# Down projections of a split-precision block: one 512-column product in place of two of 256

## The reference, cut to what matters

```python
def swiglu(x, w_gate, w_up, w_down):
    return (jax.nn.silu(x @ w_gate) * (x @ w_up)) @ w_down
...
def first_block(x, ...):
        h = rms_norm(x, ffn1_norm[l])
        x = x + FFN_RESIDUAL_WEIGHT * swiglu(h, ffn1_w_gate[l], ffn1_w_up[l], ffn1_w_down[l])   # f1u, f1d
...
        h = rms_norm(x, ffn2_norm[l])
        x = x + FFN_RESIDUAL_WEIGHT * swiglu(h, ffn2_w_gate[l], ffn2_w_up[l], ffn2_w_down[l])   # f2u, f2d
    return rms_norm(x, final_norm)
...
def second_block(x, mem, ...):
        fn = rms_norm_2(h, norm_ffn[l])
        g = fn @ ffn_w_gate[l]
        ...
        h = h + (jax.nn.silu(g_conv) * (fn @ ffn_w_up[l])) @ ffn_w_down[l]                      # f3u, f3d
    return h
```

## Time and profile before

| | before |
|---|---|
| median of 3 runs | 965.79 us |
| the profiled execution | 965.9 us |
| its span, first to last instruction | 964.2 us |
| TensorE matmul busy | 958.1 us (99%), 8272 matmuls |
| VectorE busy | 690.8 us (72%) |
| ScalarE busy | 535.0 us (55%) |
| GpSimd busy | 129.8 us (13%) |
| granted TensorE clock | 1.000 of full speed |

### The profile page before, as it was taken

The page is one execution under the profiler, slowest core; times in us unless marked ns, Lnnn a source line. Parts: engine busy times, 40 slices in busy tenths (PEclk is TensorE's granted clock), DMA queues, the critical chain, the costliest instruction groups (busy, mean ns, idle before and its releaser), DMA issues.

```text
span 964.2 us, 20474 instructions
## 1 busy us (share of the span) xinstructions
PE 958.1 (99%) x8272; PEld 941.5 (98%) x8272; DVE 690.8 (72%) x1084; ACT 535.0 (55%) x777; POOL 129.8 (13%) x85
## 2 busy tenths in 40 slices
PE   9999999999999999999999999999999999999998
PEld 8999999999999999999999999989899999999998
DVE  5767657477779968778767655697697688787752
ACT  6554454346558964456454465487575664545441
POOL 0111110010036000012111102400002032223100
PEclk9999999999999999999999999999999999999999
DMA  7775675555554544576666674345245355665761
GB/s 253 244 219 180 186 256 163 183 177 175 166 186 132 159 148 154 173 242 190 203 195 197 207 238 151 101 145 160 88 153 168 119 175 174 193 199 174 252 206 67
DMA packets 169134, 172.37 MB, mean 179 GB/s; under 512 B 5732, under 2 KB 167022, under 8 KB 168942
## 3 DMA queue, kind: packets, MB, share of 16 engines
q1 hardware_dynamic: 168238, 170.67, 55.6%
q10 hardware_dynamic: 832, 0.79, 0.3%
HBM read 170.39 MB, written 1.06 MB: 178 GB/s over the span
## 4 chain that ended last, share of the span: by engine, by line
PE 94%; DVE 2%; issue 1%; POOL 1%; DMA 1%; ACT 0%; SPq 0%; DVEq 0%; POOLq 0%
PE acc L759 84%; PE part L806 1%; PE acc L806 1%; DVE wl L476 1%; PE part L846 1%; PE part L870 1%; DMA xraw<-in_x 1%; PE part L1154 1%; PE part L856 1%; POOL sq L2815 1%; PE part L1144 0%; PE part L1350 0%; PE part L1331 0%; PE part L892 0%; PE part L1177 0%
## 5 line engine op out<-in xcount | busy, mean ns | idle before, releaser
L457 ACT ACTIVATE wh<-raw 128x1024 fp32r<-128x1024 f32 (+2 forms) x291 | 316.1, 1111 | 270.8 <-PE acc L759 115.2
L476 DVE TENSOR_TENSOR wl<-raw,wh 128x1024 fp32r<-128x1024 f32 (+2 forms) x292 | 390.6, 1378 | 53.1 <-ACT wh L457 52.6
L759 PE MATMUL acc<-ah,wh 128*128 128x256 f32 x1520 | 422.8, 279 | 0.5 <-DVE wl L476 0.3
L759 PE MATMUL acc<-ah,wl 128*128 128x256 f32 x1520 | 419.0, 277 | 0.0
L759 PE MATMUL acc<-al,wh 128*128 128x256 f32 x1520 | 415.8, 277 | 0.0
L759 PEld LDWEIGHTS acc<-ah,wh 128*128 128x128 f32 x1520 | 285.2, 188 | 4.0 <-issue 3.0
L759 PEld LDWEIGHTS acc<-ah,wl 128*128 128x128 f32 x1520 | 285.4, 188 | 0.0
L759 PEld LDWEIGHTS acc<-al,wh 128*128 128x128 f32 x1520 | 283.5, 188 | 0.1
L2834 POOL TENSOR_TENSOR sil<-sil,rstd 128x512 f32<-128x512 f32 x33 | 60.9, 1846 | 302.1 <-ACT sil L1458 213.1
L759 PE MATMUL acc<-hh,wh 128*128 128x256 f32 x352 | 97.3, 277 | 0.0
L759 PE MATMUL acc<-hh,wl 128*128 128x256 f32 x352 | 97.2, 276 | 0.0
(11 more groups left out here) (450 smaller groups left out, 1528.2 us busy)
## 6 DMA issues: line engine op xcount, KB each, us to landing
raw<-in_ffn_w_down SPq DMA_DIRECT2D x24, 1408.0 KB, 6.3
raw<-in_w_in SPq DMA_DIRECT2D x33, 1024.0 KB, 5.3
raw<-in_ffn_w_gate SPq DMA_DIRECT2D x32, 1024.0 KB, 5.4
raw<-in_ffn_w_up SPq DMA_DIRECT2D x32, 1024.0 KB, 5.3
raw<-in_w_out SPq DMA_DIRECT2D x8, 1024.0 KB, 5.0
raw<-in_w_proj_attn SPq DMA_DIRECT2D x4, 1024.0 KB, 4.9
raw<-in_w_proj_mlstm SPq DMA_DIRECT2D x4, 1024.0 KB, 5.5
raw<-in_xa_w_kv SPq DMA_DIRECT2D x4, 1024.0 KB, 5.0
```

The source lines that it names most:

```text
L457: nc.scalar.activation(wh[:, slot, a * nw:b * nw], raw[:, slot, a * nw:b * nw], ACT.Copy).then_inc(S("w_hi"), 1)
L476: nc.vector.tensor_tensor(wl[:, slot, a * nw:b * nw], raw[:, slot, a * nw:b * nw], f(wh[:, slot, a * nw:b * nw]), SUB).then_inc(S("w_lo"), 1)
L759: ins = mm(dst, a, b, start=st and q == 0, stop=en_ and q == sweep[-1], skip_group_check=True)
```

## The change

The halves `wh`, `wl` become two parts of one tensor `w_both`, and `hh`, `hl` of `h_both`. In the down projections (all but the last quarter of f3d) one matmul streams 512 moving columns: the high and the low part side by side, against the same stationary operand. Its output fills a whole bank: the left 256 columns get high x high, the right 256 high x low. The third matmul (256 columns, with the low part of the other operand) is added to the left half. So a quarter now needs two banks, one for each m, and the two halves of a bank are added at the residual, by two VectorE instructions in a row. Banks are regrouped for that, the copies of the input to `xT` move from the start of f1d to the first step of f1u, and TensorE waits for them ahead of f1d.

```diff
+        two_accs, two_sides, two_more = (ctx.enter_context(nc.psum_tensor(n, [P, 1024], f32)) for n in ("acc", "part0", "part1"))
+        DOWN = (two_sides, two_accs, two_sides, two_more)
...
+            def paired_product(s, banks, k0, tokens, kick=None):
+
+                slot = s % 2
+                for half, (ka, kb) in enumerate(halves(11)):
+                    lo_ready(pe, s, 0, half)
+                    for k in range(ka, kb):
+                        if kick is not None and kick[0] == k:
+                            mm(kick[1][0:32, 0:T], wh[:, slot, k * 256:k * 256 + 32], hh[:, k0 + k, :],
+                               start=True, stop=True, skip_group_check=True)
+                        for m in range(2):
+                            o = banks[:, m * 512:(m + 1) * 512]
+                            if tokens:
+                                c, t = slice(k * 256, (k + 1) * 256), slice(m * P, (m + 1) * P)
+                                wide = hh[:, k0 + k, t], w_both[:, :, slot, c]
+                                rest = hl[:, k0 + k, t], wh[:, slot, c]
+                            else:
+                                c = slice(k * 256 + m * P, k * 256 + (m + 1) * P)
+                                wide = wh[:, slot, c], h_both[:, :, k0 + k, :]
+                                rest = wl[:, slot, c], hh[:, k0 + k, :]
+                            mm(o.rearrange("p (a t) -> p a t", a=2), *wide, start=k0 + k == 0, stop=False, skip_group_check=True)
+                            ins = mm(o[:, 0:T], *rest, start=False, stop=k0 + k == FC - 1, skip_group_check=True)
+                    ins.then_inc(S("w_used"), 1)
...
-                        product(s + 2 * q + r, 0, 11, n + q, hh, hl, k0=11 * r, first=r == 0, last=r == 1, tokens=tokens,
-                                narrow=(1, Q[0]) if (st, q, r) in (("n1", 0, 1), ("n3", 1, 0)) else None)
+                        if (st, q, r) == ("n1", 0, 0):
+                            pe.wait_ge(*signal("x_ok", 4))
+                        if (st, q, r) == ("n3", 3, 0):
+                            pe.wait_ge(*signal("mem_lo", 2))
+                        paired_product(s + 2 * q + r, DOWN[q], 11 * r, tokens,
+                                       kick={("n1", 0, 1): (1, Q[3]), ("n3", 1, 0): (0, L[0])}.get((st, q, r)))
...
-                        V.scalar_tensor_tensor(pairs(xT, q), L[(n + q) % 2][:, :], 0.5, pairs(xT, q),
+                        side = DOWN[q][:, :].rearrange("p (m a t) -> p m a t", m=2, a=2)
+                        link(V.scalar_tensor_tensor(xT[:, 2 * q:2 * q + 2, :], side[:, :, 1, :], 0.5, xT[:, 2 * q:2 * q + 2, :], MUL, ADD))
+                        V.scalar_tensor_tensor(xT[:, 2 * q:2 * q + 2, :], side[:, :, 0, :], 0.5, xT[:, 2 * q:2 * q + 2, :],
                                                MUL, ADD).then_inc(free_sem(n + q), 1)
```

More of the change, by code:

```diff
@@ L156, in build @@
         half = sb("half", [P, 16])
-        wh = sb("wh", [P, 2, SLAB], f32r)
-        wl = sb("wl", [P, 2, SLAB], f32r)
+        w_both = sb("w_both", [P, 2, 2, SLAB], f32r)
+        wh, wl = w_both[:, 0], w_both[:, 1]
         rest = sb("rest", [P, 16])
@@ L271, in build @@
         with ExitStack() as sc:
-            hh = sb("hh", [P, FC, T], f32r, scope=sc)
-            hl = sb("hl", [P, FC, T], f32r, scope=sc)
+            h_both = sb("h_both", [P, 2, FC, T], f32r, scope=sc)
+            hh, hl = h_both[:, 0], h_both[:, 1]
             sil = sb("sil", [P, 512], scope=sc)
@@ L310, in build @@
                 probT3 = sb("probT3", [P, 2, 512], scope=s1)
-        L = [ctx.enter_context(nc.psum_tensor(f"acc{i}", [P, 512], f32)) for i in range(2)]
-        Q = [ctx.enter_context(nc.psum_tensor(f"part{i}", [P, 512], f32)) for i in range(6)]
+        two_accs, two_sides, two_more = (ctx.enter_context(nc.psum_tensor(n, [P, 1024], f32)) for n in ("acc", "part0", "part1"))
+        L = [two_accs[:, i * 512:(i + 1) * 512] for i in range(2)]
+        Q = [two_sides[:, 0:512], two_more[:, 0:512], two_more[:, 512:1024]]
+        Q += [ctx.enter_context(nc.psum_tensor(f"part{i}", [P, 512], f32)) for i in (3, 4)]
+        Q.append(two_sides[:, 512:1024])
+        DOWN = (two_sides, two_accs, two_sides, two_more)
         ident = cst[:, C_ID:C_ID + P]
@@ L792, in last_columns @@
             def last_columns(s, n):
-                banks = (L[n % 2], Q[5])
+                banks = (L[n % 2], Q[1])
                 for r in range(2):
@@ L1050, in memory_in @@
                     pe.wait_ge(*signal("mem_in", 16))
-                    transpose_in(memraw, "mem_ps", Q[2:6])
+                    transpose_in(memraw, "mem_ps", Q[1:5])
             feed_forward("f2u", "f2d", "n3", between=memory_in)
@@ L1464, in body @@
                     A_(rpair(hh, i), hid[:, :], ACT.Copy).then_inc(S(up + "_hh"), 1)
+                    if st == "n1" and isinstance(i, int) and i == 0:
+                        for j in range(4):
+                            act.wait_ge(*signal("n1_lo", j + 1))
+                            A_(pairs(xT, j), X_BANKS[j][:, :], ACT.Copy).then_inc(S("x_ok"), 1)
                 if st != "n1":
@@ L1555, in copies_and_sines @@
             def copies_and_sines(q):
-                if q == 0:
-                    for j in range(4):
-                        A_(pairs(xT, j), X_BANKS[j][:, :], ACT.Copy).then_inc(S("x_ok"), 1)
                 if q != 3:
@@ L1672, in memory_hi @@
                         for c in range(2):
-                            ins = A_(mo[:, 2 * j + c, :], Q[2 + j][:, c * T:(c + 1) * T], ACT.Copy, scale=col(V_MEM + 2 * j + c))
+                            ins = A_(mo[:, 2 * j + c, :], Q[1 + j][:, c * T:(c + 1) * T], ACT.Copy, scale=col(V_MEM + 2 * j + c))
                         ins.then_inc(S("mem_hi"), 1)
@@ L2071, in rows_added @@
                 s, n, c = SLAB0["f3d"] + 2 * q + 1, ACC0["f3d"] + q, slice(q * 256, (q + 1) * 256)
[L2072 removed]
+                side = DOWN[q][:, :].rearrange("p (b a c) -> p b a c", b=TB, a=2)
                 if q == 0:
@@ L2080, in rows_added @@
                     slab_used(dve, s)
-                    V.tensor_tensor(xtok[:, :, c], acc, xtok[:, :, c], ADD).then_inc(free_sem(n), 1)
+                    link(V.tensor_tensor(xtok[:, :, c], side[:, :, 1, :], xtok[:, :, c], ADD))
+                    V.tensor_tensor(xtok[:, :, c], side[:, :, 0, :], xtok[:, :, c], ADD).then_inc(free_sem(n), 1)
                     return
```

4 lines of the change are left out of this document (2 added, 2 removed).

## The result

The changed kernel takes 973.3 us, the median of 9 runs (lowest 972.9), against 965.5 us for the kernel before, 9 runs on the same chip: a ratio of 1.007 (95% interval 1.005 to 1.009). So it is slower, by 7.8 us, and lies above the predicted range of 962 to 971 us. Single executions reach 972.5 us before and 976.4 us after, so medians are compared. The profiled execution took 973.3 us with a span of 971.5 us; the one before had a span of 964.2 us.

A forecast was written before the change was run, and what follows sets the result against it. TensorE's product stream was taken to bound the kernel. Products at +1.6 us and the uncovered addition after f1d at +0.75 us gave +2.35 us on 965.9 us: 968.2 us, range 962.0 to 971.0 us.

The forecast's parts named there:

- What bounds the kernel: Whole run: TensorE holds 94% of the chain; f1d is busy throughout at clock 1.00, no wait.
- The wide product: Down stages: each product of 512 columns costs 230 ns, bounds 216 and 235.
- rival B: Down stages: 512 columns cost 226.7 ns, two fast products; only the wait after f1d is left, 966.6 us; chance 0.18.
- The narrow product: Down stages: the remaining product of 256 columns stays at 113.3 ns; 117.5 if slow.
- The cadence that is carried on: wq and `last_columns`: products behind a slow mixed stream stay slow; counted as nothing, 0.9 us at the upper end.
- The extra addition after f1d: Residual after f1d: the second VectorE addition has no cover and delays TensorE by 0.75 us.
- The copies in f1u and the new waits: f1u, ahead of f1d, and last quarter of f2d: cost nothing; copies at most 0.8 us without cover.
- The rest of the change: Outside the priced terms: nothing added; no term for a later `prob` between f2d and f3d.
- Rival A: Down stages: wide product streams clean at 216 to 220 ns, weight load hidden; 961.5 to 963.4 us; chance 0.28.
- The place of the short product: f2d: the short product issued directly behind the transposes, not six products later; the forecast gave no price.
- Rival C: Down stages: mixed lengths keep every product slow, 230 to 235 and 117.5 ns; 971.2 to 973.7 us; chance 0.12.
- a relation of the stream to its own weight loads: TensorE's stream: equal products can lock into a slow (117.5 ns) or fast (113.3 ns) relation to their weight loads.

The follow-up runs named there:

- experiment 2: Changed kernel with products of 512 columns split into two of 256, except the first in each of the three down stages: 972.3 us, ratio 1.006.
- experiment 1: Changed kernel with every product of 512 columns issued as two of 256 again, all else kept: 968.1 us, ratio 1.003.
- the last run of experiment 6: As experiment 1, with the short product of f2d one block later, where it stood before, adding zeros from a previously unused 64-byte tensor: 967.5 us, ratio 1.001.
- experiment 4: Kernel before the change, without its two short products (32 stationary columns) in f1d and f2d: 966.8 us, ratio 1.001.
- experiment 3: Changed kernel with the products of each half slab grouped by length, all of 512 columns first, then all of 256: 969.3 us, ratio 1.004.

## Why the prediction was wrong, by its own steps

- **What bounds the kernel: right.** TensorE's stream holds the chain before and after, at clock 1.00. Of what was added, about 1 us is TensorE's waits for other engines (after f1d, and at `prob`); the rest lies in the products.
- **The wide product, "I take 230": too low by 5 ns, 2.4 us over 484.** The earlier trace rows were read rightly in the mean (the steps of 220 and 240 are 226 to 235 in the nanoseconds of the same records), but in ukv wide products follow wide ones; alternating with narrow ones the wide product sits at 235, the upper bound that I had made of two slow products. Behind a fast stream it costs 225 to 228 ns, once per stage or group. That is two fast products, rival B's number, and true for one instruction only.
- **The narrow product, "I take 113.3, since f1d and f2d run fast when they begin": this is the step that failed most.** It measures 118.4 ns in f1d and 118.7 over all: 5.1 ns x 484 = 2.5 us at the least. The reason given was no reason. How a stage begins says nothing about it once the first wide product is in it: experiment 2 shows one wide product, 228 ns long, at the end of a fast stream, and 525 slow products behind it. With both terms the pairs cost 6.5 us in place of 1.6.
- **The cadence that is carried on, "in the sum it counts nothing": it counts 0.7 us.** 0.2 in the first slab of wq, 0.5 in `last_columns` (5.62 - 5.40, 15.44 - 14.90). The first 0.2 only fill time in which TensorE would have waited; some 0.1 more lie in the slow products behind the gap. My upper bound was 0.9.
- **The extra addition after f1d, 0.75 us: right.** 0.71 us where the stream stays as it was (experiment 1), 0.50 in the changed kernel, because the slow first slab hides a part. After f2d it cost nothing in the changed kernel, but the cover is thin: in the last run of experiment 6 TensorE is 0.3 us late there.
- **The copies in f1u and the new waits, nothing: right as far as the profile tells.** The changed kernel reaches f1d 0.8 us earlier than the kernel before.
- **The rest of the change, nothing: too low by 0.4 us.** The prediction has no term for VectorE's later `prob` between f2d and f3d. Each of the traces named above has it; which line of the diff brings it stays open.
- **Rival A's reason is not borne out.** It had the weight load out of the way after half of a wide product. In experiment 2 the load behind the wide product at 905.39 starts 5 ns after it and takes 187 of the 228 ns, more than half.
- **The place of the short product: missed.** I listed it under the diff and gave it no price. It costs 1.7 us as soon as the stream is otherwise fast (f2d in experiment 1 against f2d in the last run of experiment 6).
- **Rival C had the mechanism.** It gave 971.2 to 973.7 us for 230 to 235 ns, narrow products at 117.5 and the cadence carried on; the time is 973.3. That it falls inside is in part luck, since the 0.8 us gained ahead of f1d and the 0.4 us at `prob` were in no sum. I gave it 0.12 because the fast form came back "within a few products" in the earlier trace rows. There it came back behind a short product, not by itself: experiment 4 takes the short product away and the whole rest of the stage stays slow. That was the misreading. Behind that short product stood equal lengths, too. The 272-column products of the earlier trace rows came out of a fast stream and were slow at once, and spoke for C; but products of 256 columns behind them, with eight transposes between, went at 113 ns again (226.22 us), so they were no proof of it.

What stays open: why unequal lengths push the stream into the slow form. The prediction spoke of a relation of the stream to its own weight loads; in the kernel before each load starts 2 to 5 ns behind the start of a product in the slow stream (571.1 us) and 3 to 4 in the fast one (142.0 us), which does not show one. The 4-byte shift shows that the addresses of the operands change the distance, but with other steps than the slow form, so a common cause is not shown. The pages of the profile show only starts and durations, and neither the grouping (narrow products recover in f1d and f2d, and in f3d some groups do) nor the single wide product in f3d (they don't, for 525 products) follows from one simple rule that I could state.

## What to carry to other kernels

A dense stream of fp32r products has two speeds here, 113 and 118 ns for 256 columns (with its operands where both kernels have them), at the same clock and without any wait. Whoever changes lengths, order or addresses in it should compare start-to-start distances first; counting instructions and columns tells nothing of these 4%. Before merging two products into one of twice the length, look at the price of a *neighbour* of the long product, in a run of its own, since one wide product slowed the 525 others of f3d while being cheap itself. And price every line of a diff that puts an instruction at another place in the stream: this one moved a small product by six places, for 1.7 us.

## What the runs showed of the hardware that was not expected

- **One instruction sets the speed of hundreds behind it.** One product of 512 columns (228 ns) at the start of f3d: 62.2 us for the stage in place of 59.9.
- **Four bytes cost 3%.** Moving the activations in SBUF by 4 bytes makes each of the 8272 matmuls some 3.5 ns slower on average, 995.2 against 967.5 us, nothing else changed. The Trainium skill, page "SBUF — State Buffer", section "Door 1: The DMA port swizzle (why `[64,N]` ≈ `[32,N]`)", says that SBUF has lines of 16 bytes and that each access that crosses to a new line pays a penalty. The shift could fit that, since it changes where each row begins within such a line, but no run here shows that this is the cause: the page names no price for TensorE's operands, and shifts of 16 bytes were not tried.
- **A product of 32 stationary columns can turn the stream fast, or not.** Six products behind the transposes of f2d it does, and gives 1.6 us; directly behind them it doesn't; of nine others in a slow stream one did.
- **The slow form comes by itself, too.** In the profiled execution of experiment 3 all of f3u (862 products) ran at 117.4 ns, 3.8 us longer than otherwise, with no edit near it. It begins right behind a wait of TensorE (from 806.19 to 806.74 us). The profiles of experiments 1, 2 and 4 have the same wait, 0.55 to 0.56 us from start to start, and are fast again some six products behind it; why this one is not stays open.
